# Splitting three of the eight last updates of x between the scalar engine and GpSimd

## The reference, cut to what matters

```
f = jnp.square(jax.nn.relu(h @ w_ff1[l])) @ w_ff2[l]
x = x + gt2 * _rmsnorm(f, g_post_ffn[l])
```

## Time and profile before

| | us |
|---|---|
| median of 3 runs | 1786.08 |
| lowest and highest of them | 1785.97, 1788.33 |
| the profiled execution's own time | 1786.64 |
| its span, first to last instruction | 1785.0 |

### The profile page before, as it was taken

One profiled execution on the slowest core, in us unless ns is written; L12 is line 12 of the kernel. 1 busy time (PEld: TensorE's weight loads), 2 busy tenths in 40 slices (PEclk: granted clock), 3 DMA queues, 4 the chain that ended last, 5 costly groups with the idle time before them and its releaser, 6 DMA issues.

```text
span 1785.0 us, 25525 instructions
## 1 busy us (share of the span) xinstructions
PE 1769.9 (99%) x8242; PEld 1454.6 (81%) x8242; DVE 1259.2 (71%) x1691; ACT 895.0 (50%) x1267; POOL 124.1 (7%) x217
## 2 busy tenths in 40 slices
PE   8999999999999999999999999999999999999998
PEld 7777778887888888888888888888888888888886
DVE  5677779778877867787777868777775654545545
ACT  6866675555445454544444545444444444444443
POOL 1011101010000000110010101000000000000000
PEclk9999999999999999999999999999999999999999
DMA  9778788655667778699999966999998775655554
GB/s 348 253 262 283 240 278 313 203 183 181 205 214 253 237 221 286 204 317 318 304 305 303 317 211 224 327 311 318 311 293 240 235 222 191 196 190 194 193 190 140
DMA packets 195053, 446.93 MB, mean 250 GB/s; under 512 B 17088, under 2 KB 27312, under 8 KB 194608
## 3 DMA queue, kind: packets, MB, share of 16 engines
q1 hardware_dynamic: 166544, 342.23, 58.9%
q0 software_dynamic: 28304, 103.89, 17.4%
q10 hardware_dynamic: 144, 0.03, 0.0%
HBM read 434.03 MB, written 12.06 MB: 250 GB/s over the span
## 4 chain that ended last, share of the span: by engine, by line
PE 95%; DMA 2%; DVE 1%; ACT 1%; SPq 0%; issue 0%; DVEq 0%; ACTq 0%
PE bank L1579 30%; PE bank L1581 30%; PE bank L1580 30%; DMA raw<-in_w_in_a 2%; PE bank L1625 1%; PE bank L1749 1%; PE bank L1732 1%; DVE w_lo L1001 0%; PE bank L1724 0%; PE bank L1842 0%; PE bank L1848 0%; PE bank L1721 0%; DVE x L1028 0%; PE bank L1605 0%; ACT y L594 0%; PE bank L1854 0%
## 5 line engine op out<-in xcount | busy, mean ns | idle before, releaser
L1001 DVE TENSOR_TENSOR w_lo<-raw,w_hi 128x1024 fp32r<-128x1024 f32 x605 | 728.8, 1210 | 412.2 <-ACT w_hi L590 409.9
L590 ACT ACTIVATE w_hi<-raw 128x1024 fp32r<-128x1024 f32 x605 | 633.5, 1050 | 712.0 <-PE bank L1581 644.1
L1579 PE MATMUL bank<-w_hi,h_hi 128*128 128x512 f32 x2272 | 896.2, 394 | 3.7 <-DVE w_lo L1001 2.4
L1581 PE MATMUL bank<-w_hi,h_lo 128*128 128x512 f32 x2272 | 885.8, 390 | 0.0
L1580 PE MATMUL bank<-w_lo,h_hi 128*128 128x512 f32 x2272 | 885.1, 390 | 0.0
L1579 PEld LDWEIGHTS bank<-w_hi,h_hi 128*128 128x128 f32 x2272 | 426.9, 188 | 95.8 <-issue 5.3
L1581 PEld LDWEIGHTS bank<-w_hi,h_lo 128*128 128x128 f32 x2272 | 426.6, 188 | 89.8
L1580 PEld LDWEIGHTS bank<-w_lo,h_hi 128*128 128x128 f32 x2272 | 427.1, 188 | 85.2
L515 POOL DMA_DIRECT2D ada_raw<-in_w_ada x160 | 84.7, 530 | 953.1 <-DVE acc_a L1008 709.8
L1008 DVE SCALAR_TENSOR_TENSOR acc_a<-ada_raw,cond,acc_a 128x1024 f32<-128x1024 f32 x112 | 143.3, 1280 | 10.8 <-DMA ada_raw<-in_w_ada 10.7
L1008 DVE SCALAR_TENSOR_TENSOR acc_b<-ada_raw,cond,acc_b 128x1024 f32<-128x1024 f32 x48 | 64.3, 1340 | 1.5 <-DMA ada_raw<-in_w_ada 1.4
(11 more groups left out here) (209 smaller groups left out, 934.6 us busy)
## 6 DMA issues: line engine op xcount, KB each, us to landing
raw<-in_w_ff SPq DMA_DIRECT2D x256, 512.0 KB, 4.7
raw<-in_w_in SPq DMA_DIRECT2D x176, 512.0 KB, 4.6
ada_raw<-in_w_ada POOLq DMA_DIRECT2D x160, 512.0 KB, 5.5
raw<-in_w_in_a SPq DMA_DIRECT2D x69, 512.0 KB, 5.0
ada_more<-in_w_ada POOLq DMA_DIRECT2D x32, 512.0 KB, 5.7
raw<-in_w_out_a SPq DMA_DIRECT2D x32, 512.0 KB, 5.6
raw<-in_w_o SPq DMA_DIRECT2D x32, 512.0 KB, 5.2
raw<-in_w_moba SPq DMA_DIRECT2D x16, 512.0 KB, 5.6
```

Of the source, the lines that this page charges most:

```text
L590: act.activation(used(w_hi, turn, s), used(raw, turn, s), ACT.Copy).then_inc(hi_ready, 1)
L1001: dve.tensor_tensor(used(w_lo, turn, s), used(raw, turn, s), used(w_hi, turn, s).bitcast(F32), ALU.subtract).then_inc(lo_ready, 1)
L1579: pe.matmul(out_ap, hi, rhs_hi, start=start, stop=False)
L1581: return pe.matmul(out_ap, lo, rhs_hi, start=False, stop=stop)
```

## The change

For pieces (0,2), (0,3) and (1,3) the vector engine's update is taken out. In its place the scalar engine scales `y2` in place by `y_rstd` (an activation Copy with a scale for each partition), and GpSimd adds the result to x. The vector engine keeps (0,0), (0,1), (1,0), (1,1) and (1,2). The sync engine still issues the eight transfers in the order of the pieces, and waits for the new semaphore `x_added` for three of them.

```diff
+        BY_POOL = ((2, 3), (3,))
...
             for t in range(T):
                 for c in range(CHUNKS):
-                    sp.wait_ge(x_new, (2 * T + t) * CHUNKS + c + 1)
+                    if c in BY_POOL[t]:
+                        sp.wait_ge(x_added, t * len(BY_POOL[0]) + BY_POOL[t].index(c) + 1)
+                    else:
+                        sp.wait_ge(x_new, 2 * T * CHUNKS + t * (CHUNKS - len(BY_POOL[0])) + c + 1)
                     sp.dma_start(out_tiles[:, t, c * CH:(c + 1) * CH], x[:, t, c * CH:(c + 1) * CH]).then_inc(stored, 16)
...
+            for n, (t, c) in enumerate((t, c) for t in range(T) for c in BY_POOL[t]):
+                pool.wait_ge(y_normed, n + 1)
+                piece = x[:, t, c * CH:(c + 1) * CH]
+                pool.tensor_tensor(piece, y2[:, t, c * CH:(c + 1) * CH], piece, ALU.add).then_inc(x_added, 1)
...
                     act.activation(y_rstd[:, t:t + 1], y_sq[:, t, c:c + 1], ACT.Sqrt, bias=y_var[:, t:t + 1],
                                    scale=1.0 / D).then_inc(y_root, 1)
+                    act.wait_ge(y_root, 2 * (2 * T + t) + 2)
+                    for q in BY_POOL[t]:
+                        act.wait_ge(y_scaled, t * CHUNKS + q + 1)
+                        part = y2[:, t, q * CH:(q + 1) * CH]
+                        act.activation(part, part, ACT.Copy, scale=y_rstd[:, t:t + 1]).then_inc(y_normed, 1)
...
-            def add_residual(r, t, y):
+            def add_residual(r, t, y, others=()):
...
                 for c in range(CHUNKS):
+                    if c in others:
+                        continue
                     piece = x[:, t, c * CH:(c + 1) * CH]
...
-                    add_residual(3, t, y2)
+                    add_residual(3, t, y2, BY_POOL[t])
```

More of the change, by code:

```diff
@@ L250, in two_block_kernel @@
         x_new = sem("x_new")
+        y_normed = sem("y_normed")
+        x_added = sem("x_added")
         x_squared = sem("x_squared")
```

## The result

The changed kernel takes 1791.22 us (median of 12 runs, 1788.49 to 1793.2) against 1785.66 us for the kernel before (median of 12). The ratio is 1.0026, 95% interval 1.0017 to 1.0034, so 3.0 to 6.1 us slower (the quotient of the two medians, 1.0031, lies inside the interval). I had forecast 0.6 us slower.

A forecast was written before the change was run, and what follows sets the result against it. The tensor engine bounds 95% of the span; only the stage behind the last matrix product can move. Span 1785.0 + 0.0 + 0.6 = 1785.6 us; against the median, 1786.08 + 0.6 = 1786.7 us, range 1785.1 to 1788.3.

The forecast's parts named there:

- 1.32 us taken off ahead of tile 1: Two tile 0 updates leave the vector engine; as it then waits for squares, only 0.39 us reaches tile 1.
- The copies: Scaled copies on the scalar engine, 0.70 us each (bounds 0.63 and 0.80), making the last square 0.19 us later.
- The addition's first run: GpSimd's first tile 0 addition: 1.4 us with a wait of 0.3 for update (0,1), at no cost.
- The second addition: GpSimd's other tile 0 addition: 1.4 us beside gain products of 0.68 us, which would not be held.
- Update (1,2) was held: Tile 1: GpSimd's addition delays this vector update by 1.04 us, giving back all of the 0.39 + 0.66 us.
- the forecast 0.6 us: At the end, the last two pieces are issued 0.33 us apart through full DMA engines: last landing 0.6 us later.
- A: GpSimd and the vector updates run side by side, nothing is held: 0.5 us faster, 1785.6 us; chance 0.10.
- B: Vector engine keeps its turn: update (1,2) runs before the waiting GpSimd, last issue 0.1 us later, 1786.2 us; chance 0.15.
- C: GpSimd starts cold, its first addition late by 0 to 29.5 us, so slower; chance 0.05, half beyond 0.2%.
- D: Instruction fetching or the start shifts, or the split fails to do what it says; no size; chance 0.08.
- The exclusion of the two engines: Vector instructions with two SBUF inputs and GpSimd instructions reading SBUF exclude each other whole; tile 1 hold of 1.04 us.

The follow-up runs named there:

- the run with one piece: The split for piece (0,3) alone, against the kernel before: ratio 1.0006 (0.9997 to 1.0015), 1787.19 us.
- the run with the fill: Changed kernel with a DRAIN behind GpSimd's last transfer issue and zeros written for (1,3) instead of the addition (wrong output): ratio 0.9999, 1786.72 us.
- the run with the wait alone: The kernel before plus one wait for the last update of x at the end of GpSimd's program, no arithmetic: ratio 1.0028, 1791.43 us.

## Why the prediction was wrong

In the sum it is the term that was missing: the DRAIN ends 1.89 (first update) + 0.79 (copy, signal) + 1.73 (addition) + 7.4 = 11.8 us behind the last matrix product, which sets the end at 12.1 and not at 8.5. That is 4.2 us over before in the profiles; the measured ratio says 3.0 to 6.1. The forecast had given 0.95 to a change under 0.2% (3.6 us), on the ground that less could hardly be told; the interval came out at 1.5 us to either side, and the change at 0.26%.

**The steps that held.** Of the 1.32 us taken off ahead of tile 1, 0.34 reached it (0.39 forecast), since the squares then set the pace. The copies took 0.72 us (0.70). The addition's first run was 1.77 us: 1.4 and a wait of 0.37 for update (0,1). The second addition, 1.29 us, ran beside gain products of 0.69 us, none of which was held. Update (1,2) was held by 3.08 - 2.08 = 1.00 us (1.04), which ate the rest: the last update ended 4.97 us behind the last matrix product, before 4.96. The transfers then cost the forecast 0.6 us. The split without a DRAIN at the end and the one with an early DRAIN, at 8.5 and 8.4, show this sum by itself.

**The rivals.** A fell with the length of update (1,2), B with the order: GpSimd, which had waited, went first. C was the right side with the wrong mechanism. GpSimd did not start cold; its first addition in 1000 us began 0.09 us after the copy (1772.50 + 0.72 to 1773.31). Its program ended late; it did not begin late. The Trainium skill, GPSIMD Engine Reference, section Instruction dispatch, gives about 6 us for the first call of a freshly loaded kernel; no run shows any of it at these additions, and GpSimd had made its subtractions long before them. D, "something else", had 0.08 and no size; it should have been broken up by asking what is the last instruction on each engine.

**The exclusion of the two engines** was read from four earlier subtractions and met three times: on (1,2) here, on (0,2) in the run with one piece, and as GpSimd's own wait. The Trainium skill, SBUF — State Buffer, section Who interferes with whom, says so too, and that a GpSimd instruction which only writes SBUF does not contend with a vector instruction of two SBUF inputs; the run with the fill agrees (2.08 us for three updates).

## What to carry to other kernels

Work that is moved to an engine that had already finished moves that engine's closing instruction too: look at what each engine does between its last work and the end of the program before giving a long idle one something to do late. Where GpSimd has issued many transfers, put a DRAIN into an idle stretch behind the last of them, or give it no late work. Read such a cost from the last instructions of each engine: the chain that ended last stopped 7 us before the end here, and the wait named the wrong engine. And an update with two SBUF inputs on the vector engine and an addition on GpSimd are not parallel work: here the hold of 1.0 us took all that the split had gained.

## What the hardware showed that I had not expected

- GpSimd's DRAIN lasts 0.082 us for each transfer that it has issued since its last DRAIN: 2.7 us behind 32, 4.5 behind 54, 5.6 behind 68. With 134 and 202 it is 7.4. The transfers had landed long before (in the run with the wait alone their last packet ended at 1322.6, 459 us ahead of the DRAIN), so it is not their landing. What it does in that time, and why it stops growing, stays open.
- The Trainium skill, VectorE: DVE Perf Modes, section The DRAIN you can't avoid, gives about 12 ns for the DRAINs that the runtime puts ahead of and behind a program, on all five engines. Those at line 105 belong to the kernel's own block, so that figure need not hold for them: the sync engine's took 7 ns, GpSimd's 7.4 us behind its last work.
- Two instructions of the vector engine in a row do not keep GpSimd out: an addition that waits gets in between them, and the second waits 1.0 us.
